# A two-layer encoder step: mixer operations and weight pieces in the orders of VectorE and ScalarE, and the place of the attention scores among seven products

## What is computed

```python
qa, ka, va, g = jnp.split(h @ w_in, N_PROJ, axis=-1)
q = rms_norm(qa.reshape(bn, t, N_HEADS, HEAD_DIM), q_w)
k = rms_norm(ka.reshape(bn, t, N_HEADS, HEAD_DIM), k_w)
z = jnp.einsum('bqhd,bkhd->bhqk', q, k) * (HEAD_DIM ** -0.5)
log_one_minus = jnp.where(earlier, jax.nn.log_sigmoid(-z), 0.0)
between = lax.cumsum(log_one_minus, axis=3, reverse=True) - log_one_minus
w = jnp.where(earlier, jnp.exp(jax.nn.log_sigmoid(z) + between), 0.0)
o = jnp.einsum('bhqk,bkhd->bqhd', w, v)
x = x + (o * jax.nn.silu(g)) @ w_out
```

## Time and profile before

| | before |
|---|---|
| median of 3 runs | 2485.13 us (2481.74 to 2487.21) |
| profiled execution | 2485.89 us, span 2484.2 us, clock 0.954 |
| TensorE busy | 2303.8 us, 93% |
| VectorE busy | 1617.5 us, 65% |
| ScalarE busy | 1143.0 us, 46% |
| GpSimd busy | 73.3 us, 3% |

### The profile page before, as it was taken

The page is one execution under the profiler, slowest core; times in us unless marked ns, Lnnn a source line. Parts: engine busy times, 40 slices in busy tenths (PEclk is TensorE's granted clock), DMA queues, the critical chain, the costliest instruction groups (busy, mean ns, idle before and its releaser), DMA issues.

```text
span 2484.2 us, 44785 instructions
## 1 busy us (share of the span) xinstructions
PE 2303.8 (93%) x17257; PEld 2265.7 (91%) x17257; DVE 1617.5 (65%) x2647; ACT 1143.0 (46%) x1552; POOL 73.3 (3%) x75
## 2 busy tenths in 40 slices
PE   7788888988888889889999999999999999998999
PEld 7788888878878889888999999999999999998999
DVE  7776677667657766674234777777777777778221
ACT  5645445544445454454224444454444444545221
POOL 5000000000000000003110000000000000000000
PEclk9889899889889898999999999999999999999999
DMA  7322222222222222253544222222222222221442
GB/s 265 96 86 70 82 74 80 82 70 81 71 86 86 86 72 79 86 161 89 146 131 111 79 72 79 71 79 79 72 78 76 74 75 77 74 67 47 135 124 79
DMA packets 394498, 225.26 MB, mean 91 GB/s; under 512 B 9523, under 2 KB 378726, under 8 KB 394342
## 3 DMA queue, kind: packets, MB, share of 16 engines
q1 hardware_dynamic: 344342, 189.83, 26.9%
q10 hardware_dynamic: 50032, 33.81, 4.3%
HBM read 195.04 MB, written 28.56 MB: 90 GB/s over the span
## 4 chain that ended last, share of the span: by engine, by line
PE 65%; DVE 15%; issue 9%; ACT 7%; ACTq 1%; DVEq 0%; DMA 0%
PE psum L666 45%; PE psum L873 6%; ACT w_hi L1018 5%; PE psum L656 3%; PE psum L789 2%; PE psum L712 2%; ACT work L1018 1%; DVE work L1586 1%; DVE sp_lo L1604 1%; DVE sp_lo L1617 1%; DVE qk_lo L1576 1%; PE psum L738 1%; DVE w_chain L1468 1%; DVE w_chain L1476 1%; DVE qk_lo L1556 1%
## 5 line engine op out<-in xcount | busy, mean ns | idle before, releaser
L666 PE MATMUL psum<-act_hi,w_hi 128*128 128x272 f32 x3200 | 678.7, 293 | 15.0 <-DVE act_lo L1542 5.3
L666 PE MATMUL psum<-act_lo,w_hi 128*128 128x272 f32 x3200 | 662.8, 289 | 0.0
L666 PE MATMUL psum<-act_hi,w_lo 128*128 128x272 f32 x3184 | 661.1, 289 | 0.0
L1018 ACT ACTIVATE w_hi<-w_raw 128x1024 fp32r<-128x1024 f32 x350 | 367.7, 1055 | 509.0 <-PE psum L666 256.4
L666 PEld LDWEIGHTS psum<-act_hi,w_hi 128*128 128x128 f32 x3200 | 504.5, 189 | 17.7 <-POOL act_lo L640 5.5
L666 PEld LDWEIGHTS psum<-act_lo,w_hi 128*128 128x128 f32 x3200 | 505.4, 189 | 0.0
L666 PEld LDWEIGHTS psum<-act_hi,w_lo 128*128 128x128 f32 x3184 | 500.1, 190 | 0.0
L1450 DVE TENSOR_TENSOR w_lo<-w_raw,w_hi 128x1024 fp32r<-128x1024 f32 x199 | 250.2, 1258 | 305.1 <-ACT w_hi L1018 305.0
L1018 ACT ACTIVATE work<-work 128x544 f32<-128x544 f32 (+6 forms) x336 | 235.5, 733 | 284.2 <-DVE work L1697 189.1
L1456 DVE TENSOR_TENSOR w_lo<-w_raw,w_hi 128x1024 fp32r<-128x1024 f32 x150 | 183.6, 1224 | 226.8 <-ACT w_hi L1018 226.8
L873 PE MATMUL psum<-act_hi,w_hi 128*128 128x272 f32 x960 | 289.7, 302 | 6.5 <-issue 5.5
(11 more groups left out here) (271 smaller groups left out, 3255.7 us busy)
## 6 DMA issues: line engine op xcount, KB each, us to landing
w_raw<-in_w_in SPq DMA_DIRECT2D x241, 512.0 KB, 4.0
w_raw<-in_w_out SPq DMA_DIRECT2D x64, 512.0 KB, 6.5
out<-work ACTq DMA_DIRECT2D x48, 256.0 KB, 2.4
x_residual<-work ACTq DMA_DIRECT2D x32, 272.0 KB, 3.7
work<-x_residual SPq DMA_DIRECT2D x32, 272.0 KB, 3.1
w_chain<-in_w_in SPq DMA_DIRECT2D x15, 512.0 KB, 4.1
full<-x_residual SPq DMA_DIRECT2D x8, 544.0 KB, 7.9
o_spill<-work ACTq DMA_DIRECT2D x15, 272.0 KB, 2.1
```

The costliest lines, as they stand in the source:

```text
L666: mm = pe.matmul(acc[par][:, j, :], at, a[:, k, j * HT:(j + 1) * HT], start=(k == 0 and n == 0), stop=(k == KT - 1 and n == 2))
L1018: return nc.scalar.activation(out, in_, f, **kw)
```

## The change

It moves operations in three lists; no operation is added or taken out.

- TensorE: `att_scores` stands after product 4 instead of product 3.
- VectorE: the normalisation of q and k (cases 1 and 2 before) stands in step 1; the split of the normalised q and k (`qk_lo`, case 3 before) at the end of step 2, ahead of piece 5 (`piece_lo` of step 3); `sp_lo` and `later_lo` (case 8) in step 7, between `piece_lo` and `weight_sum`; the split of the attention weights (case 11) at the end of step 10; and the split of the next head's squares (case 0) in step 13, right behind the head's output, no longer in step 0 of the next head. For head 0 it stands ahead of the loop.
- ScalarE: `qk_hi` is case 2 alone; the gate's three operations are case 3; absolute value, exponential and logarithm of the scores stand together in step 5, the copies of k and v and the gate's last exponential in step 6.
- The tables of the last head follow.

```diff
@@ -881,7 +881,7 @@
                         product(i, n * HEAD_PIECES + s)
                         if s == 0:
                             att_sums_and_turns(i * BODY + n)
-                        elif s == 3:
+                        elif s == 4:
                             att_scores(i * BODY + n)
                         elif s == 9:
                             att_cumulated(i * BODY + n)
@@ -1100,29 +1100,29 @@
                     ch.wait()
                     func(qk_sq, qk_sq, ACT.Exp, scale=-0.5).then_inc(qk_rstd, 1)
                 elif s == 2:
+                    act.wait_ge(qk_normed, h + 1)
+                    func(qk_hi, qkn, ACT.Copy).then_inc(qkn_hi_ready, 1)
+                elif s == 3:
                     act.wait_ge(evacuated, h * 4 + 4)
                     ch.done(func(g_tmp, Y[:, 3, :], ACT.Abs))
                     ch.wait()
                     ch.done(func(g_tmp, g_tmp, ACT.Exp, scale=-1.0))
-                    act.wait_ge(qk_normed, h + 1)
-                    func(qk_hi, qkn, ACT.Copy).then_inc(qkn_hi_ready, 1)
                     ch.wait()
                     func(g_tmp, g_tmp, ACT.Ln, bias=one_c[:]).then_inc(gate_log, 1)
-                elif s == 3:
                     act.wait_ge(v_copied, h + 1)
                     act.dma_start(v_prompt_v[:, :, bass.ds(h, 1), :].rearrange("p b h d -> p b (h d)"), v_nat[:, 0:NB, :]).then_inc(v_stored, 16)
                     act.dma_start(v_sample[0, 0][:, bass.ds(h, 1), :].rearrange("p h d -> p (h d)"), v_nat[SROW:P, 4, :]).then_inc(v_stored, 16)
-                elif s == 4:
+                elif s == 5:
                     act.wait_ge(stage_b, h + 1)
                     ch.done(func(za[:, 0:512], M[0], ACT.Abs))
                     ch.done(func(za[:, 512:896], M[1][:, 0:384], ACT.Abs))
                     ch.done(func(za[:, 896:Z_ALL], M[2][:, 0:480], ACT.Abs))
-                    func(k_nat[:, 0:NB, :], M[3].rearrange("p (b d) -> p b d", b=NB), ACT.Copy).then_inc(k_copied, 1)
                     ch.wait()
                     ch.done(func(za, za, ACT.Exp, scale=-1.0))
-                elif s == 5:
                     ch.wait()
                     func(za, za, ACT.Ln, bias=one_c[:]).then_inc(soft_log, 1)
+                elif s == 6:
+                    func(k_nat[:, 0:NB, :], M[3].rearrange("p (b d) -> p b d", b=NB), ACT.Copy).then_inc(k_copied, 1)
                     func(v_hi, v_nat[:, 0:3, :], ACT.Copy).then_inc(v_hi_ready, 1)
                     act.wait_ge(gate_ls, h + 1)
                     func(g_tmp, g_tmp, ACT.Exp).then_inc(gate_sig, 1)
@@ -1370,7 +1370,7 @@
                         if l == 1:
                             act.wait_ge(o_ready, l * H + H - 1)
                     elif l == 0:
-                        for s in ((1, 2), (3, 4), (5,), (7,), (), (10,), (11,))[u]:
+                        for s in ((1, 2), (3,), (5, 6), (7,), (), (10,), (11,))[u]:
                             att_act(H - 1, s)
                     else:
                         rec_act(H - 1, u)
@@ -1561,7 +1561,6 @@
                     ch.done(dve.tensor_copy(v_nat[:, 0:NB, :], M[3].rearrange("p (b d) -> p b d", b=NB)))
                     dve.wait_ge(past_copied, h + 1)
                     dve.tensor_copy(v_nat[:, 4, :], M[2][:, 64:192]).then_inc(v_copied, 1)
-                elif s == 2:
                     if not (isinstance(h, int) and h == 0):
                         dve.wait_ge(k_stored, h * 32)
                     dve.wait_ge(qk_rstd, h + 1)
@@ -1570,7 +1569,7 @@
                                                      op0=ALU.mult, op1=ALU.mult))
                     dve.scalar_tensor_tensor(out=kn, in0=Y[:, 1, :], scalar=WK, in1=qk_sq[:, 1, :],
                                              op0=ALU.mult, op1=ALU.mult).then_inc(qk_normed, 1)
-                elif s == 3:
+                elif s == 2:
                     dve.wait_ge(qkn_hi_ready, h + 1)
                     dve.wait_ge(qk_normed, h + 1)
                     dve.tensor_tensor(qk_lo, qkn, qk_hi.bitcast(F32), ALU.subtract).then_inc(qkn_lo_ready, 1)
@@ -1632,14 +1631,18 @@
                             piece_lo(i, off + 2)
                         else:
                             lo(OUT_BASE[0] + off + 2 - BODY_PIECES, off + 2 - BODY_PIECES)
-                        if s in (3, 8):
-                            att_dve(i * BODY + n, s)
+                        if s == 7:
+                            att_dve(i * BODY + n, 8)
                         if not (last_turn(i) and off + 3 >= BODY_PIECES):
                             weight_sum(i, off + 3)
                         if s:
                             fast_add(i, off - 1)
-                        if s not in (3, 8):
+                        if s == 10:
+                            att_dve(i * BODY + n, 11)
+                        elif s not in (0, 8, 11):
                             att_dve(i * BODY + n, s)
+                        if s == 13:
+                            att_dve(i * BODY + (n + 1), 0)
                     fast_add(i, off)
 
 
@@ -1933,6 +1936,7 @@
                     piece_lo(0, 1)
                     weight_sum(0, 2)
                     evacuate(0, 0, 3)
+                    att_dve(0, 0)
                     for m in range(4):
                         a = slice(2 * m, 2 * m + 2)
                         dve.wait_ge(diff_hi_ready, 8 + m + 1)
@@ -1983,7 +1987,7 @@
                     if l == 1 and u == 6:
                         rec_output(H - 1)
                     if l == 0:
-                        for s in ((0,), (1, 2), (3, 4), (), (6,), (8, 9), (), (11,), (13,))[u + 1]:
+                        for s in ((), (1,), (2, 4), (), (6,), (8, 9), (), (11,), (13,))[u + 1]:
                             att_dve(H - 1, s)
                         if u == -1:
                             lo(g0 + 2, 2)
```

## The result

The changed kernel takes **2275.1 us** (median of 4 runs, 2273.8 to 2278.8), beside 2486.2 us (2481.7 to 2490.8) for the kernel before on the same chip: ratio 0.915 (95% interval 0.913 to 0.917), 211 us less. The forecast was 2271, a gain of 214. The profiled execution took 2275.1 us, its span is 2273.4 (before 2484.2), the mean clock 0.994 (before 0.954).

The account below looks back on a forecast made before the run. It took the stage as a dense TensorE program with holes, waits for VectorE that also lower the clock. Stage 1012.0 less 810.8, plus 7.6 earlier start and 5 in the tail, gave 214 us: 2271, range 2255 to 2310.

Parts of the forecast that it names:

- start of the stage: First head's sums: with the squares' split ahead of six splits of differences, they begin 7.6 us earlier.
- stage: From the first head's sums to the tail's sums: 810.8 us, against 1012.0 before.
- TensorE's own work: One head without waits at full clock: fourteen products, sums, scores, cumulated sums and mixing take 52.9 us.
- Product 9's wait: Product 9 of each head: due at 29.4, it waits 0.4 us for its piece's low half, ready at 29.8.
- Spares: Time in hand before TensorE needs an input in a head: 4 us at the scores, 2.6 at product 8, 0.5 at product 10.
- The branches: Loop's branch: its 2.0 us wait stays, giving four heads of 55.3 us beside nine of 53.3.
- The first and the last head: Ends of the stage: the first head takes 56.5 us, 3.2 more for pieces behind six splits; the last 53.4.
- The tail's 5: Tail: output splits ahead of the softplus remove a 5.21 us wait, some returns; gain 5, between 0 and 7.
- A: Sums and scores: mixer work itself lowers the clock, so only the waits go; 2353 us, chance 6%.
- B: Weight pieces 4, 8, 9 or 10: waits move there, 3 us a head, half the clock's loss returns; 2348 us, 8%.
- C: Whole stage: dense work on TensorE, ScalarE and VectorE lowers the clock, making the kernel slower, 2685 us; chance 3%.
- D: Sums: the late input is the past keys' load, or pieces take up the rest; time within 0.2%, chance 2%.

Follow-up runs that it names:

- mended kernel: Changed kernel with VectorE's scaling of half of one sum done one sum later and the tail's spill loads 1 to 3 held until the past keys landed: 2259.7 us.
- filled waits: Kernel before with 24 dummy products in each of TensorE's two waits per head, ahead of sums and scores, no operation moved: 2411.9 us, ratio 0.968.

## Why the prediction was right

It was right in sign, size and mechanism; its total is 214 us against 211, and 4 us of time.

| term | forecast | in the profiles |
|---|---|---|
| start of the stage | 7.6 earlier | 9.2 earlier |
| stage | 810.8 us | 812.8 us |
| behind the tail's sums | 5 | 2.3 (1375.9 before, 1373.6 after) |
| sum | 213.8 | 210.8 |

- **TensorE's own work, 52.9 us a head.** With no wait at all a head takes 52.57 (mended kernel), so the term was 0.3 too large. Most of that is the scores: the 3.3 us were read to the end of the last matmul, in a stretch with a wait behind it; from their start to the next product's they take 3.03.
- **Product 9's wait of 0.4** was 0.51 and made a head 0.77 longer. Both errors together: 53.34 against 53.3.
- **Spares.** At the scores 4 us were placed, 3.06 measured. That 3 of them come from the product the scores were moved behind is right; of the 1 us left to the order, 0.05 was there, and with the scores back it was just enough. The narrowest cover, product 10's, held. The sums' spare was 1.0 by hand, 1.09 measured.
- **The branches.** The forecast counted four, of 2.0 each. There are three: the way out of the loop into the last turn cost nothing (53.34). But one of the three was followed by a fall of the clock, and that head took 57.2, the other two 55.3 and 55.5. The miscount and the fall nearly cancel (701.5 us for the thirteen middle heads, forecast 700.9). The forecast had this fall in its upper bound only.
- **The first and the last head.** The first took 56.12, forecast 56.5. The last took 55.1, 1.7 more than forecast, since the tail's sums wait 4.56 us for the past keys where they waited 2.96.
- **The tail's 5** is the term furthest off for its size. The output's splits are early, as said: the wait of 5.21 is 0.5 now. But 1.40 came back at the softplus, and behind the longer wait for the keys the clock fell, which the sums paid with 1.65 (3.53 us from 899.80 to the next product at 903.33, against 1.88) and the product behind them with 0.5. That the term left out the transfers was the error. The keys are now issued 3.0 us behind the third of the spill's loads, where it was 6.0 (the two pairs of rows below, now and before), and land in 7.3 us instead of 5.8. The run in which the spill's loads wait shows that these loads are the cause: the keys land in 2.7 us and the wait is gone. The stage's length alone does not set how they meet: the wait is 4.60 with the squares back (stage 887 us) and 2.28 with ScalarE's order back (844).

```profile
889.19 3.12 SPq L510 DMA_DIRECT2D full<-o_spill  x1
...
892.21 0.39 ACTq L1086 DMA_DIRECT2D past<-in_cache_k  x1
```

```profile
1096.36 4.39 SPq L510 DMA_DIRECT2D full<-o_spill  x1
...
1102.32 0.39 ACTq L1086 DMA_DIRECT2D past<-in_cache_k  x1
```

- **The start.** The wait fell from 9.66 to 2.38, 7.3, against 7.6. The other 2 us are the beginning of the program, which varies: the first sums lie between 87.1 and 91.2 in the ten profiles with the early split.

The rivals: A is refuted by the filled waits and by the changed kernel's own sums and scores (1.81 and 3.03 us); the sums with their seven turns ran at 1.00. The rule cited beside it (the Trainium skill, "TensorE: Matmul & The Clock Gate", Part 4: PE-mode transpose: transposes do not count as work for the clock the way matmuls do) did not show here, with seven turns among six other matmuls. B came only as the 0.51 at product 9. C is excluded: the densest stretches ran at 1.00. Its price was also too low: the 4.58 us were not a product at the lower level, since the clock was back at full for the last 1.3 of them (666.80 to 668.06 in the kernel before). Matmuls at the lower level start 0.227 us apart there, so a product wholly at it takes some 5.4, a head some 94 and the kernel some 2870 us (an estimate from these distances and the forecast's 17 us of mixer work). D is excluded in the loop; in the tail, its condition, the late past keys, does hold.

What the prediction did not see is how the parts hang together. It took each part's wait as its gain. On the chip the scores' move and the softplus' run cancel, and the parts undone one at a time cost 19, 41, 20, 85, 31 and 5 us, 201 in all by the medians and 170 by the ratios: a sum that need not meet the 211, and that by the medians comes near it by chance. The forecast's total was not reached in that way, so its agreement does not rest on this; but its errors did cancel in two places, within a head and at the branches.

## What to carry to other kernels

Read a wait on TensorE together with the clock of the work behind it: here 88 of 199 us were the clock's, and cutting one hole of 3.3 us a head into two of 1.5 and 1.1 gave 61 us with idle time 9.5 us less. Test a change of several moves by undoing pairs as well as single moves: two moves that each look worth 20 to 40 us may only pay for each other. When the work ahead of a transfer moves, look at the end of the stage for transfers that now meet there.

## What was not expected of the hardware

Whether the clock falls behind a wait of 2 to 3 us varies from one pass to the next. Behind the branch's wait of 2.10 us it fell in the changed kernel (first row), behind those of 1.69 and 1.92 it did not; over ten of these kernels, 12 of 30 branches of 1.7 to 2.2 us were followed by a fall, though not in step with their length: it fell behind 1.79 and 1.83, and stayed up behind 2.13. Fifteen waits of 1.7 to 2.0 before the cumulated sums, with `sp_lo` back, were followed by none; in the filled kernel one of fifteen such waits was, the one of 2.00. All fourteen waits of 2.8 to 4.7 before the sums of the later heads, with the squares back, were followed by a fall. But waits of the same length are not always: in the kernel before, the clock stayed up behind four of the fourteen waits before these sums (2.55 and three of 3.08) and behind one of the fifteen at the scores, of 3.26 (third row), and in the kernel with the scores' move alone behind five of the fourteen before the sums (2.54 to 3.08). The second row is the tail's sums behind their wait of 4.56.

```profile
249.00:252.40 3.40, 3.31 (x14) 3.32 (x15) 0.55 (x3) 1.06 (x1) 0.00 (x0) 0.51 0.14 47
```

```profile
899.80:902.80 3.00, 3.00 (x10) 2.61 (x11) 0.00 (x0) 0.00 (x0) 1.26 (x1) 0.50 0.29 36
```

```profile
1064.30:1067.70 3.40, 3.38 (x28) 3.25 (x29) 3.01 (x4) 1.06 (x1) 0.00 (x0) 1.00 0.71 200
```

What sets the waits with a fall apart from those without was not tested and stays open.
